# Layer 0's pooling and differential-attention mixer rebuilt: both maps' scores issued together, projections by halves of a bank, q and k turned by on-chip DMA

## The reference, cut to what matters

```python
q = apply_rope(rms_norm(q, q_g), cos, sin)   # per map, 64 wide; k likewise
...
    s = jnp.einsum('bhcqd,bhckd->bhcqk', qi, k) * scale
    s = jnp.where(kpos[None, :] <= qpos[:, None], s, NEG_INF)
    p = jax.nn.softmax(s, axis=-1)
    w = p[:, :, 0] - lam * p[:, :, 1]
    return jnp.einsum('bhqk,bhkd->bhqd', w, vf)
...
o = rms_norm(o, subln_g) * (1.0 - lam_init)
return jnp.concatenate([a, b], axis=-1) @ w_out     # a is the pooling branch
```

## Time and profile before

| what | us |
|---|---|
| median of 3 runs | 2597.24 |
| lowest, highest | 2586.86, 2598.13 |
| span of the profiled execution | 2591.6 |
| head 0 begins (first scores) | 88.7 |
| heads 1, 2, 3 begin | 181.4, 280.0, 375.6 |
| last pooling matmul starts | 477.4 |

### The profile page before, as it was taken

One profiled execution on the slowest core, in us unless ns is written; L12 is line 12 of the kernel. 1 busy time (PEld: TensorE's weight loads), 2 busy tenths in 40 slices (PEclk: granted clock), 3 DMA queues, 4 the chain that ended last, 5 costly groups with the idle time before them and its releaser, 6 DMA issues. The chain is left out here.

```text
span 2591.6 us, 27736 instructions
## 1 busy us (share of the span) xinstructions
PE 2479.0 (96%) x10664; PEld 1923.1 (74%) x10664; DVE 1472.3 (57%) x1359; ACT 568.0 (22%) x836; POOL 894.6 (35%) x401
## 2 busy tenths in 40 slices
PE   6899898899999999999988999999999999999998
PEld 5566565687777777878856777777877777777786
DVE  6454556535666666666666324434466666666667
ACT  5233332311111111111133323332211111111111
POOL 2111112273333333333353123225533333333332
PEclk8898999999999999999988999999999999999999
DMA  3000000211111111111120011103111111111111
GB/s 141 17 17 17 17 21 25 90 49 41 49 45 44 49 49 49 49 41 48 54 98 33 25 33 41 33 25 114 41 49 49 49 40 49 49 49 46 43 49 73
DMA packets 34192, 122.83 MB, mean 47 GB/s; under 512 B 3920, under 2 KB 4304, under 8 KB 34128
## 3 DMA queue, kind: packets, MB, share of 16 engines
q1 hardware_dynamic: 31680, 113.29, 13.1%
q10 hardware_dynamic: 2448, 8.65, 0.9%
HBM read 113.54 MB, written 8.39 MB: 47 GB/s over the span
## 5 line engine op out<-in xcount | busy, mean ns | idle before, releaser
L1235 POOL TENSOR_TENSOR w_hi<-w_raw,ones 128x1024 fp32r<-128x1024 f32 x188 | 361.7, 1924 | 1643.7 <-PE pj L260 751.5
L1146 DVE TENSOR_TENSOR res<-dn,res 128x1024 f32<-128x1024 f32 x352 | 430.8, 1224 | 281.5 <-PE dn L1051 271.6
L1237 POOL TENSOR_TENSOR w_lo<-w_raw,w_hi 128x1024 fp32r<-128x1024 f32 x188 | 466.4, 2481 | 14.8
L1095 DVE SCALAR_TENSOR_TENSOR ffn_y<-ffn_h,params,ffn_y 128x1024 f32<-128x1024 f32 x176 | 295.4, 1678 | 150.1 <-ACT ffn_y L1103 138.7
L1103 ACT ACTIVATE ffn_y<-ffn_h,params 128x1024 f32<-128x1024 f32 x88 | 109.6, 1246 | 1046.5 <-DVE ffn_h L1084 1046.5
L1051 PE MATMUL dn<-act_hi_buf,w_hi 128*128 128x512 f32 x704 | 235.5, 416 | 9.2 <-DVE res L1146 6.7
L1051 PE MATMUL dn<-act_lo_buf,w_hi 128*128 128x512 f32 x704 | 219.9, 394 | 0.0
L1051 PE MATMUL dn<-act_hi_buf,w_lo 128*128 128x512 f32 x704 | 219.5, 393 | 0.0
L1034 PE MATMUL pj<-xa_hi,w_hi 128*128 128x512 f32 x704 | 217.4, 390 | 0.0
L1034 PE MATMUL pj<-xb_hi,w_hi 128*128 128x512 f32 x704 | 217.3, 390 | 0.0
L1034 PE MATMUL pj<-xa_hi,w_lo 128*128 128x512 f32 x704 | 217.0, 389 | 0.0
(11 more groups left out here) (245 smaller groups left out, 3356.0 us busy)
## 6 DMA issues: line engine op xcount, KB each, us to landing
w_raw<-weights SPq DMA_DIRECT2D x189, 512.0 KB, 3.4
x_first<-x_t SPq DMA_DIRECT2D x8, 512.0 KB, 9.0
res<-x_t SPq DMA_DIRECT2D x8, 512.0 KB, 6.5
scratch<-res ACTq DMA_DIRECT2D x8, 512.0 KB, 2.6
res<-scratch SPq DMA_DIRECT2D x8, 512.0 KB, 7.5
y_t<-res ACTq DMA_DIRECT2D x8, 512.0 KB, 2.6
consts<-consts SPq DMA_DIRECT2D x2, 320.0 KB, 7.3
pos_int<-positions SPq DMA_DIRECT2D x1, 512.0 KB, 11.3
```

Of the source, the lines that this page charges most:

```text
L1095: dve.scalar_tensor_tensor(y[:, :], h[:, SH - lag:SH - lag + S], f.tap(j, m, q), y[:, :], ALU.mult, ALU.add).then_inc(taps[f.l], 1)
L1146: dve.tensor_tensor(res[:, d, :], dn[:, d % 2, :], res[:, d, :], ALU.add).then_inc(dn_free[d % 2], 1)
L1235: pool.tensor_tensor(whi[:, w, :], raw[:, r, :], ones[:, 0:1].to_broadcast([P, D]), ALU.mult).then_inc(w_high, 1)
L1237: pool.tensor_tensor(wlo[:, w, :], raw[:, r, :], whi[:, w, :].bitcast(F32), ALU.subtract).then_inc(w_ready, 1)
```

## The change

- Scores: one call per block issues, for each 512 columns of keys, the matmul of map 0 (partitions 0 to 63) and then that of map 1 (partitions 64 to 127), into different banks. Blocks 0 to 3 alternate between two pairs of banks; from block 4 on each map has two banks of its own. All four banks of `dn` now hold scores; `xt` (transposes), `po` and `ojunk` move to `pj`'s second half.
- Projections: only `pj`'s first half is left for them. A tile is made by halves of 512 positions: eight units of six matmuls, all six into one bank, the first four units for half 0. Evacuations, VT, OT and PW go by halves as well.
- q and k: q's rms factor is no longer applied to q. It multiplies the score rows in the pass that also takes the minimum (the factor is negated), and the exponential has scale -1. q and k, unnormed, are multiplied by gain and cosine; a copy with the 32-partition halves exchanged, made by four DMAs on SP's queue (`sp_turn`, before the loads of tiles 5, 6, 8, 9, 11, 12, 14, 15), is multiplied by gain and sine; then the sum. k's rms factor is widened by ACT, transposed by PE (`pe_KB`, four transposes a half) and multiplied onto k. The row matmuls (L384), the spreading (L393) and the rotation (L398) are gone; the sums of squares stay, in two parts (`pe_stat_qk`).
- Combining: the factor of map 1 relative to map 0 is computed on one column; one pass makes `w_combined`; map 0's factor is applied by ACT when it copies PV.
- Order: per block one group, transposes, the middle groups, transposes, one group, PV. In the last block of a head `pe_KB` stands before and after the scores, and VT's halves between the last transposes and before PV. In the prologue q and k are evacuated ahead of the tables. `ORDER0` and `EARLY0` of the output tiles change from 4 to 5 early slices.

```diff
+        def half(*key):
+            half_job[key] = len(half_job)
+        for t in range(2):
+            half("q", 0, t)
+        for key in (("v", 0, 0), ("v", 0, 1), ("KB", 0, 0), ("KB", 0, 1), ("VT", 0, 0), ("VT", 0, 1)):
+            half(*key)
+        for g in range(1, HEADS):
+            for key in (("q", g, 0), ("q", g, 1), ("k", g, 0), ("k", g, 1), ("v", g, 0), ("KB", g, 0), ("KB", g, 1),
+                        ("v", g, 1), ("VT", g, 0), ("VT", g, 1)):
+                half(*key)
+        for key in (("u", 0), ("u", 1), ("PW", 0), ("u", 2), ("PW", 1), ("u", 3), ("PW", 2), ("PW", 3)):
+            for t in range(2):
+                half(*key, t)
...
+        def pe_unit(pe, n, kind, g, u, X):
+            t, part = divmod(u, 4)
+            key = (kind, g, t)
+            if u == 0:
+                pe.wait_ge(w_ready, n + 1)
+            o = half_take(pe, key) if part == 0 else bank(key)
+            wsl = n % W_RING
+            for k in (2 * part, 2 * part + 1):
+                a, b = whi[:, wsl, k * P:(k + 1) * P], wlo[:, wsl, k * P:(k + 1) * P]
+                for m, (w, x) in enumerate([(a, X[0]), (a, X[1]), (b, X[0])]):
+                    ins = pe.matmul(o, w, x[:, k, t * HALF:(t + 1) * HALF],
+                                    start=(k == 0 and m == 0), stop=(k == KC - 1 and m == 2))
+            if u == 3:
+                ins.then_inc(first_half, 1)
+            elif u == 7:
+                ins.then_inc(tile_done, 1)
...
+        def sc_at(i, c):
+            return 2 * HALF * (i % 2) + HALF * c if i < 4 else 2 * HALF * c
+        def pe_stat_qk(pe, g, m):
+            pe.wait_ge(qk_sq, 2 * g + m + 1)
+            xt_take(pe, ("ST", g, m))
+            for i in range(TB):
+                ins = pe.matmul(xt[:, 2 * i:2 * i + 2], (sqq, sqk)[m][:, i * P:(i + 1) * P], selq[:, 0:2], start=True, stop=True)
+            ins.then_inc(xt_full, 1)
...
+        def act_wide(act, g):
+            act.wait_ge(st_dve, g + 1)
+            act.wait_ge(roped, g + 1)
+            if g:
+                act.wait_ge(kb_pe, 2 * g)
+            r = 32 * (g % 2) + 16
+            src = rstd[:, r:r + 16].rearrange("p (i a) -> p i a", a=1).to_broadcast([P, 16, QKD])
+            act.activation(rkb[:, :].rearrange("p (i a) -> p i a", i=16), src, ACT.Copy).then_inc(wide, 1)
+        def pe_KB(pe, g, t):
+            key = ("KB", g, t)
...
+        def pe_KB(pe, g, t):
+            key = ("KB", g, t)
+            pe.wait_ge(wide, g + 1)
+            o = half_take(pe, key)
+            for i in range(4):
+                ins = pe.transpose(o[:, i * P:(i + 1) * P], rkb[:, (4 * t + i) * P:(4 * t + i + 1) * P], ident)
+            ins.then_inc(kb_pe, 1)
+        def dve_KB(dve, g, t):
+            key = ("KB", g, t)
+            dve.wait_ge(kb_pe, 2 * g + t + 1)
+            dve.wait_ge(k_sum, g + 1)
+            dst = kf[:, g % 2, t * HALF:(t + 1) * HALF]
+            half_done(dve.tensor_tensor(dst, dst, bank(key), ALU.mult), key)
...
+        def dve_turned(dve, g, m):
+            dve.wait_ge((q_rot, k_rot)[m], 64 * (g + 1))
+            if g == 0:
+                dve.wait_ge(tabs, 2)
+            t = (qr, kr)[m]
+            link(dve, dve.scalar_tensor_tensor(t[:, :], t[:, :], (gqr, gkr)[m][:, 0:1], sinT[:, :], ALU.mult, ALU.mult))
+        def dve_straight(dve, g, m):
+            dst = (qf, kf)[m][:, g % 2, :]
+            if g >= 2:
+                dve.wait_ge(scores_done, 8 * (g - 1))
+            link(dve, dve.scalar_tensor_tensor(dst, (qz, kz)[m][:, :], gq8[:, 0:1] if m == 0 else pc(PC_KG), cosT[:, :],
+                                               ALU.mult, ALU.mult))
+        def dve_rope_sum(dve, g, m):
+            dst = (qf, kf)[m][:, g % 2, :]
+            dve.tensor_tensor(dst, dst, (qr, kr)[m][:, :], ALU.add).then_inc((roped, k_sum)[m], 1)
...
+        def sp_turn(sp, g, m):
+            src, dst = ((qz, qr), (kz, kr))[m]
+            if g == 0 and m:
+                sp.wait_ge(k0_free, 1)
+            else:
+                half_evacuated(sp, ("qk"[m], g, 0))
+                half_evacuated(sp, ("qk"[m], g, 1))
+            if m:
+                xt_filled(sp, ("ST", g, 0))
+                if g:
+                    sp.wait_ge(k_sum, g)
+            elif g:
+                sp.wait_ge(kb_pe, 2 * g)
+            for a in range(4):
+                b = a ^ 1
+                sp.dma_start(dst[32 * a:32 * a + 32, :], src[32 * b:32 * b + 32, :]).then_inc((q_rot, k_rot)[m], 16)
...
+        def dve_evac_first(dve):
+            dve.wait_ge(stat_act[0], 3)
+            dve.wait_ge(tile_done, 1)
+            for t in range(2):
+                half_done(dve.tensor_tensor(qz[:, t * HALF:(t + 1) * HALF], bank(("q", 0, t)), rbc[:, t * HALF:(t + 1) * HALF],
+                                            ALU.mult), ("q", 0, t))
+            dve.wait_ge(tile_done, 2)
+            dve.tensor_tensor(kz[:, :], pj[:, 1, :], rbc[:, :], ALU.mult).then_inc(k0_free, 1)
...
-        def pe_scores(pe, h, i, c):
...
+        def pe_scores(pe, h, i):
...
+                roped_k(pe, h)
                 if h == 0:
                     pe.wait_ge(stat_act[0], 3)
-            if 2 * a + c:
-                pe.wait_ge(exp_done, 2 * a + c)
+            exps = 2 * (a - 1) if i in (1, 2, 3) else 2 * a
+            if exps:
+                pe.wait_ge(exp_done, exps)
             width = P * (i + 1)
             for t in range(0, width, HALF):
                 e = min(width, t + HALF)
-                ins = pe.matmul(sc[:, t:e], qf[64 * c:64 * c + 64, h % 2, i * P:(i + 1) * P],
-                                kf[64 * c:64 * c + 64, h % 2, t:e], start=True, stop=True)
...
+            return (g[:1], [], g[1:]) if n == 2 else (g[:1], g[1:-1], g[-1:])
...
                     between, middle, after = block_groups(last, i)
-                    pe_scores(pe, h, i, 0)
+                    if i == TB - 1 and not last:
+                        pe_KB(pe, h + 1, 0)
+                    pe_scores(pe, h, i)
+                    if i == TB - 1 and not last:
+                        pe_KB(pe, h + 1, 1)
                     for G in between:
                         group(G)
                     if i:
                         pe_T(pe, h, i - 1, 0)
-                    pe_scores(pe, h, i, 1)
                     for G in middle:
                         group(G)
                     if i and n_groups(i - 1) == 2:
                         pe_T(pe, h, i - 1, 1)
+                    if h and i in (OT_STEP, OT_STEP + 1):
...
             act.wait_ge(maxed, 2 * a + c + 1)
-            if c == 0 and a:
+            if a:
                 act.wait_ge(combined, a)
-            if c == 1 and a:
-                act.wait_ge(transposed, groups_before(a))
             r = 2 * (a % 2) + c
-            width = P * (i + 1)
-            act.activation(pr[:, c, 0:width], sc[:, 0:width], ACT.Exp, bias=nmax[:, r:r + 1],
+            width, at0 = P * (i + 1), sc_at(i, c)
+            act.activation(pr[:, c, 0:width], sc[:, at0:at0 + width], ACT.Exp, bias=nmax[:, r:r + 1], scale=-1.0,
...
+        def dve_mask(dve, h, i):
+            a, at0 = TB * h + i, sc_at(i, 0)
+            apart = sc_at(i, 1) - at0
+            dve.wait_ge(scores_done, a + 1)
+            both = sc[:, at0:at0 + 2 * apart].rearrange("p (c t) -> p c t", c=2)[:, :, i * P:(i + 1) * P]
+            mask = cb(CB_MASK_QK).rearrange("p (a t) -> p a t", a=1).to_broadcast([P, 2, P])
+            dve.tensor_tensor(both, both, mask, ALU.add).then_inc(masked, 1)
         def dve_max(dve, h, i, c):
-            a = TB * h + i
-            r = 2 * (a % 2) + c
-            dve.wait_ge(scores_done, 2 * a + c + 1)
-            dve.tensor_tensor(sc[:, i * P:(i + 1) * P], sc[:, i * P:(i + 1) * P], cb(CB_MASK_QK), ALU.add).then_inc(masked, 1)
-            dve.wait_ge(masked, 2 * a + c + 1)
-            dve.tensor_reduce(nmax[:, r:r + 1], sc[:, 0:P * (i + 1)], AX, ALU.max, negate=True).then_inc(maxed, 1)
+            a, at0 = TB * h + i, sc_at(i, c)
+            r, col = 2 * (a % 2) + c, 32 * (h % 2) + 2 * i + c
+            dve.wait_ge(masked, a + 1)
+            s = sc[:, at0:at0 + P * (i + 1)]
+            dve.tensor_scalar(s, s, rstd[:, col:col + 1], None, ALU.mult, ALU.min,
+                              accum_out=nmax[:, r:r + 1]).then_inc(maxed, 1)
...
             dve.wait_ge(exp_done, 2 * a + 2)
             link(dve, dve.reciprocal(rinv[:, r:r + 2], rsum[:, r:r + 2]))
-            link(dve, dve.tensor_tensor(rinv[:, r + 1:r + 2], rinv[:, r + 1:r + 2], nlam[:, 0:1], ALU.mult))
-            link(dve, dve.tensor_scalar(pr[:, 1, 0:width], pr[:, 1, 0:width], rinv[:, r + 1:r + 2], None, ALU.mult))
-            dve.scalar_tensor_tensor(pr[:, 1, 0:width], pr[:, 0, 0:width], rinv[:, r:r + 1], pr[:, 1, 0:width],
+            link(dve, dve.scalar_tensor_tensor(beta[:, a % 2:a % 2 + 1], rsum[:, r:r + 1], nlam[:, 0:1], rinv[:, r + 1:r + 2],
+                                               ALU.mult, ALU.mult))
```

(56 more changed lines are left out.)

512 lines of the change are left out of this document (269 added, 243 removed).

## The result

The changed kernel takes 2470.76 us (median of 4 runs, 2469.58 to 2472.24) against 2597.68 for the kernel before beside it; the ratio is 0.9517, 95% interval 0.9495 to 0.9539. It is 126.9 us faster. The profiled span fell from 2591.6 to 2469.4, by 122.2.

What follows compares the result with a forecast made beforehand. PE's own work was taken as the bound, the score-to-transposes chain second. Terms 6.1 + 19.8 + 23.6 + 17 (idle and low clock) + 7 = 73.5 us, off 2597.2, gave 2524 us, range 2498 to 2562.

Steps and rivals of the forecast that it cites:

- scores, fixed cost: Score calls of the four heads: 64 calls become 32, at 0.19 us each, 6.1 us gone.
- scores, overlap: Score matmuls of both maps on different partitions partly run side by side: 19.8 us saved, bounds 0 and 31.
- q and k: Heads 1 to 3: row, spreading and rotation matmuls go, eight transposes come; net 7.9 us a head, 23.6 in three.
- idle: PE's waits in the four heads: double-buffered scores and VT shorten them, leaving about 24 of 34 us.
- low clock: PE's time at reduced clock in the four heads: about 18 of 25 us stays.
- prologue: Before the first scores: earlier evacuation and dropped round trips start scores at 80 to 83 us, not 88.7; 7 us, bounds 0 and 10.
- output tiles: After the last PV: the chain over norm, transposition, high and low part is the same; worth nothing.
- half-bank units: Projections by halves: same number of matmuls and weight loads, six in turn into one bank; cost nothing.
- the copies: Turned q and k by DMA: cost nothing as long as landing stays under some 8 us.
- the middle: Score overlap if two-record matmuls start in program order: 4.95 us a head, 19.8 in four; partial overlap's chance 0.45.
- rival B: Scores of both maps overlap fully: 2513 us, near 2500 if waits also vanish; chance 0.15.
- late waits: New PE waits late in each head: 5 us a head for heads 0 to 2, 6 to 9 for head 3.

Runs made afterwards that it cites:

- pe_work: The changed kernel plus 24 unused 512-column float32 matmuls on PE, ahead of k's factor transposes for heads 1 to 3: 2491.43 us, 20.7 us more.
- no_copy: The changed kernel without the on-chip copies; DVE reads raw q and k unturned, so the rotation is left out: 2472.62 us, ratio 0.9522.
- same_rows: The changed kernel with map 1's score matmuls also reading partitions 0 to 63, so map 1 is wrong: 2503.31 us, 32.5 us above the changed kernel.
- maps_apart: The changed kernel with a block's score matmuls issued map by map instead of bank by bank: 2472.03 us, ratio 0.9522.
- single_buffer: The changed kernel without the alternating score buffers of blocks 0 to 3: 2472.96 us, ratio 0.9521.
- early_pairs: The kernel before, with map 1's scores in blocks 0 to 3 given their own bank and issued right behind map 0's: 2552.0 us against 2594.6.
- slow_copy: The changed kernel with each group of four turned copies made three times in sequence, there after about 14 us: 2510.41 us, 39.6 us more.
- light_rows: The kernel before, with q and k's row, spreading and rotation matmuls cut to one block or 4 columns in heads 1 to 3: 2582.06 us against 2593.83.

## Why the prediction was wrong, step by step

The gain was split as the prediction splits it. Of the 41.9 us of scores, 6.1 + 31 = 37.1 are fixed cost and overlap, the rest low clock. The transposes lost 4.8 beyond the clock (below). What is left of the work rows, 4.8 (scores) + 11.2 + 2.1 + 1.6 (transposes) = 19.7, agrees with the 20.7 by the granted clock, though it is a remainder.

| term | predicted | measured | off by |
|---|---|---|---|
| scores, fixed cost | 6.1 | 6.1 (taken as predicted) | |
| scores, overlap | 19.8 | 31 | 11.2 |
| q and k, less 1.2 in the small rows | 23.6 | 22.9 | -0.7 |
| idle | 10 | 23.4 | 13.4 |
| low clock | 7 | 19.7 | 12.7 |
| transposes | 0 | 4.8 | 4.8 |
| prologue | 7 | 6.4 | -0.6 |
| output tiles | 0 | 4.6 | 4.6 |
| rest of the program | 0 | 3.3 | 3.3 |
| sum | 73.5 | 122.2 | 48.7 |

**Direction and large terms.** PE's own work decides: right, where `pe_work` tried it. q's and k's 23.6, the prologue and the half-bank units came near what was worked out (six matmuls of a unit mostly take 1.46 to 1.50 us from start to start behind other work and 1.39 behind another unit; a group of before at full clock takes 1.48 to 1.50), and the copies cost nothing (`no_copy`). In the prologue v starts at 46.74, as forecast; what the working left out is that DVE, which ends last, itself stands idle 8.2 us for ACT.

**What the 48.7 us are.** Idle and low clock are 26.1 of them, the overlap of the scores 11.2, the terms put at nothing 12.7, less 1.3. The overlap alone would have left the forecast at 2513, inside its range.

**Scores, overlap: the step that chose the middle failed.** The bounds were right, and the end was right that rival B named. I let an argument about two-record matmuls, that records start in the order of the program and so only one of two can lie beside the next, decide between them, with no row behind it. `same_rows` shows 31.6 us in the scores and 32.5 in the time; `maps_apart` shows map 1's records starting ahead of map 0's that stand before them. Of the pages, "TensorE: Matmul & The Clock Gate", section "Part 3: Packing small matmuls", of the Trainium skill states that matmuls on different row groups run concurrently; this case agrees, also for float32 matmuls of two records (two records in 0.70 us where one takes 0.69). The page does not say of its example how many records a matmul has; that they were single was my reading. The same section states that matmuls start in program order, on which the middle case rested; in `maps_apart` the measurement differs, and it decides.

**Idle: a wrong cause, and 13 us.** The prediction had the second buffer remove the wait for exponentials. `single_buffer` shows it worth nothing; `early_pairs` shows that a bank for each map and both issued together remove 12 of the 18 us. The late waits that I set against it, 3 x 5 and the 9 at the top of my own count, so 24, came to 11.0 in all four heads, and the longest is 1.3. These had been guessed generously rather than read: DVE and ACT have little to do in a block, and a chain of 5.8 us fits under the cover of 8 that the prediction worked out itself.

**Low clock: an effect of the idle, priced as if it were apart.** I left 18 of 25 us in place. With the waits gone the granted clock rose to 0.97 to 1.00 and 4.7 are left; the earlier trace rows had shown how a single wait of 2.79 us doubles the call behind it. The same coupling is in `early_pairs` and, with the sign turned, in `slow_copy` and `light_rows`. Idle and low clock should have moved together.

**Transposes: a term that was not there.** In the kernel before, map 1's scores stood behind most transposes; in the changed one a projection group does. Four transposes at full clock take 231.62 - 231.09 = 0.53 us from start to start ahead of a score call, and 109.65 - 109.29 = 0.36 in the changed kernel, as PE's timelines show, first of before, then of after:

```profile
231.09 0.60 PE L509 MATMUL dn<-identity,probs 128*128 128x128 f32 x4
231.62 1.55 PE L497 MATMUL dn<-k_roped,q_roped 64*128 64x512 f32 x4
```

```profile
109.29 0.60 PE L639 MATMUL pj<-identity,w_combined 128*128 128x128 f32 x4
109.65 0.47 PE L302 MATMUL pj<-xa_hi,w_hi 128*128 128x512 f32 x1
```

With 28 such places 0.17 each is 4.8 us, an estimate. "TensorEngine Tiling (Array Packing)", section "Key Properties", of the Trainium skill states that a change of tiling mode drains the array. That agrees in kind, and the price here is paid on either side of a score call: 0.19 us in the call, as the prediction took it from the earlier trace rows, and 0.17 on the transposes ahead, which it missed. That the change of rows is what costs them was not tried apart: `same_rows`, with both maps on the same 64 rows, still changes them once a call.

**Output tiles.** 4.6 us, not nothing. PE's wait for xa_lo and res there fell from 5.6 to 2.8 us. Whether that is one more early slice or a shorter end of head 3 was not tried.

**q and k: right in sum, but not for any kernel.** That 24 us of PE's line count in full holds where something else covers ACT's copies. In the kernel before, `light_rows` keeps 12 to 15 us of 22: PV's wait for `w_T` grows by 7.3 and the clock falls. On top of `early_pairs` the same removal brings 15.8 us of 22.9. The prediction read that wait (4.7) only as something that VT would shorten, not as one that the removed matmuls had been holding down.

**Range and chances.** The likeliest cases were taken one at a time. Of the 24 + 18 = 42 us of idle and low clock that the forecast left in place, full overlap "near 2500" took only 13 away. With both terms taken from the bounds (31 for 19.8, 40 for 17) the sum would have been 107.7 and the time 2490; the transposes, the output tiles and the rest, 12.7, are most of what is still missing.

## What to carry to other kernels

Two 64-deep float32 matmuls on partitions 0 to 63 and 64 to 127, in different banks and issued one behind the other, cost one of them; the pairing, with a bank for each, also takes a wait out of the middle of a block, and in `early_pairs` waits, clock and fixed cost gave more than the overlap (34 us against 8.6). Work taken off the bounding engine pays in full only if it was not also cover for a wait, so look at what stands between a producer on another engine and its consumer before it goes. And price idle and low clock as one: in these runs, where waits went, the slow calls behind them went too.

## What the runs showed of the hardware

Matmuls of the two halves of the rows run side by side record by record (two in 0.70 us), and program order across the halves does not bind (`maps_apart`, 2472.0 against 2470.8; four 512-column records have begun before a 128-column one that stands ahead of two of them in the program). A group of four 128 KB copies within the chip's SBUF, 32 partitions each, is there 4.8 us after its start, and 9 us more in each group cost 39.6 us in all, of which PE's longer waits are 24.2. A scaling pass that also takes the minimum costs 1.29 us at 1024 columns, hardly more than the plain maximum's 1.22, with an accumulator read of 0.14 behind it, here in DVE's groups of 0 to 500 us:

```profile
L986 DVE TENSOR_SCALAR_CACHE_REDUCE dn<-dn,rstd 128x1024 f32<-128x1024 f32 x8 | 10.0, 1291 | 0.1
```
